# Expert rows added in memory by an accumulating scatter, and a last stage with fused sums that scales two tiles behind

## What is computed

```python
def expert_block(args):
    xblk, ex = args
    h = jax.nn.silu(xblk @ w_gate[ex]) * (xblk @ w_up[ex])
    return h @ w_down[ex]
...
return jnp.einsum("tkd,tk->td", y_slot.reshape(T, TOP_K, D), wts.astype(y_slot.dtype))
...
y_moe = _hier_moe(u, w_rg, w_re, w_e_gate, w_e_up, w_e_down)
x = _layer_norm(DEEPNORM_ALPHA * x + gate2 * y_moe, ln_g[1], ln_b[1])
```

## Time and profile before

| what | us |
|---|---|
| median of 3 runs | 1905.53 (1901.12 to 1906.41) |
| the profiled execution's own time | 1910.53 |
| its span, first to last instruction | 1908.8 |
| mixer stage | about 40 to 930 |
| output stage with routing | about 930 to 1250 |
| expert blocks, first to last scatter issued | 1284.3 to 1785.4 |
| combine stage | 1793.5 to 1908.8 |

### The profile page before, as it was taken

The page is one execution under the profiler, slowest core; times in us unless marked ns, Lnnn a source line. Parts: engine busy times, 40 slices in busy tenths (PEclk is TensorE's granted clock), DMA queues, the critical chain, the costliest instruction groups (busy, mean ns, idle before and its releaser), DMA issues. The chain is left out here.

```text
span 1908.8 us, 29069 instructions
## 1 busy us (share of the span) xinstructions
PE 1732.3 (91%) x8892; PEld 1341.6 (70%) x8893; DVE 1162.1 (61%) x1880; ACT 619.7 (32%) x770; POOL 585.8 (31%) x679
## 2 busy tenths in 40 slices
PE   5999999999999999999689999269999999999674
PEld 2777777777888799999468877246776776776321
DVE  3676666666666666666456887744565333455298
ACT  2333333223333322222211111123565334465233
POOL 0122222111222222012144556532443333343155
PEclk7999999999999899999799999579999999999897
DMA  6443334443333231322565342379899865797595
GB/s 251 160 135 128 113 120 144 134 144 110 97 105 94 72 100 51 101 95 58 177 196 175 128 138 100 100 239 342 295 380 361 283 217 176 267 323 289 215 390 176
DMA packets 171432, 342.72 MB, mean 180 GB/s; under 512 B 18932, under 2 KB 109844, under 8 KB 166335
## 3 DMA queue, kind: packets, MB, share of 16 engines
q1 hardware_dynamic: 148518, 285.35, 44.5%
q0 software_dynamic: 18000, 55.87, 8.0%
q10 hardware_dynamic: 4818, 0.26, 0.2%
HBM read 276.86 MB, written 64.58 MB: 179 GB/s over the span
## 5 line engine op out<-in xcount | busy, mean ns | idle before, releaser
L1532 DVE TENSOR_TENSOR w_gu_lo<-w_gu_raw,w_gu_hi (+1 forms) x64 | 146.5, 2292 | 146.9 <-ACT w_gu_hi L1525 141.7
L860 DVE TENSOR_TENSOR w_lo<-w_raw,w_hi 128x1024 fp32r<-128x1024 f32 x112 | 138.6, 1241 | 137.0 <-ACT w_hi L539 134.3
L651 POOL TENSOR_TENSOR o_r<-o_ms,neg_half 128x4 f32<-128x4 f32 (+1 forms) x16 | 16.8, 1051 | 640.6 <-DVEq L914 640.6
L685 PE MATMUL pr<-ua_hi,w_hi 128*128 128x512 f32 x448 | 185.0, 413 | 10.8 <-DVE ua_lo L865 10.8
L1920 PE MATMUL py<-w_dn_w,hhT 128*128 x400 | 183.2, 601 | 11.0 <-ACT hhT L1745 6.5
L685 PE MATMUL pr<-ub_hi,w_hi 128*128 128x288 f32 (+1 forms) x672 | 189.2, 335 | 0.0
L1881 PE MATMUL ph<-w_gu_hi,x_hi 128*128 (+1 forms) x408 | 183.4, 449 | 2.5 <-DVE x_lo L1784 2.5
L685 PE MATMUL pr<-ub_lo,w_hi 128*128 128x288 f32 (+1 forms) x672 | 183.8, 327 | 0.0
L685 PE MATMUL pr<-ub_hi,w_lo 128*128 128x288 f32 (+1 forms) x672 | 183.6, 327 | 0.0
L685 PE MATMUL pr<-ua_lo,w_hi 128*128 128x512 f32 x448 | 178.8, 399 | 0.0
L685 PE MATMUL pr<-ua_hi,w_lo 128*128 128x512 f32 x448 | 178.7, 399 | 0.0
(11 more groups left out here) (334 smaller groups left out, 3432.4 us busy)
## 6 DMA issues: line engine op xcount, KB each, us to landing
w_raw<-in_w_in SPq DMA_DIRECT2D x112, 512.0 KB, 4.1
w_gu_raw<-in_w_e_gate SPq DMA_DIRECT2D x32, 1024.0 KB
w_gu_raw<-in_w_e_up SPq DMA_DIRECT2D x32, 1024.0 KB
w_dn_w<-in_w_e_down SPq DMA_DIRECT2D x32, 1024.0 KB
w_mod<-in_w_mod_rest SPq DMA_DIRECT2D x16, 1024.0 KB
y_t<-y_scratch SPq DMA_DIRECT2D x16, 1024.0 KB, 7.5
w_ring<-in_w_mod_first SPq DMA_DIRECT2D x4, 2048.0 KB, 16.4
x_cols<-in_x_prompt_t SPq DMA_DIRECT2D x32, 256.0 KB, 4.9
```

The lines of the kernel that those rows point to most:

```text
L651: pool.tensor_tensor(o_r[:, 0:c], o_ms[:, 0:c], keep["neg_half"][:, 0:c], ALU.pow).then_inc(o_rs, 1)
L685: last = pe.matmul(pr[n % 2][:, a * 512:a * 512 + c], w[:, n % WS, k, :], x[:, k, a * c:(a + 1) * c], start=(k == 0 and m == 0), stop=(k = ...
L860: dve.tensor_tensor(w_lo[:, n % WS], w_raw[:, n % WRAW], w_hi[:, n % WS].bitcast(F32), ALU.subtract).then_inc(lo_done, 1)
L1532: dve.tensor_tensor(w_slot(keep["gu_lo"], s, lo, hi), w_slot(keep["gu_raw"], r, lo, hi), w_slot(keep["gu_hi"], s, lo, hi).bitcast(F32), AL ...
```

## The change

It does the following.

- The scatter of the expert stage adds to memory (`compute_op=ALU.add`), and both rows of token n have row n of y2 as destination; y2 has 2240 rows instead of 4352. Since an accumulation needs zeros to start from, 18 transfers of up to 512 KB (`clear_sums`) write zeros in units 10 to 15 of the mixer, from a tile that DVE clears once at the end of unit 9.
- In the combine stage one 512 KB load replaces the 1024 KB one, and tiles are loaded eight ahead instead of six. The PE step is gone. DVE's weigh reads the loaded tile in SBUF. The residual is scaled and added by one DVE operation from SBUF, which gives the row sums too (`accum_out`). ACT squares the centred tile with a row sum (`spread`) where it scaled the residual before; POOL makes variance plus epsilon of it. The two statistics operations and one small column leave DVE.
- `scale` and `shift` run two tiles behind instead of one, with three `z` and two `ps_n` tiles.

```diff
+        zero_rdy, zero_out = sem("zero_rdy"), sem("zero_out")
...
+        zeros = w_mod[:, :, :].rearrange("p k n -> p (k n)")[:, 0:D]
...
+                def clear_sums(i):
+                    n = min(P, NTOK + P - i * P)
+                    sp.wait_ge(zero_rdy, 1)
+                    sp.dma_start(scr["y2"][i * P:i * P + n, :], zeros[0:n, :]).then_inc(zero_out, 16)
...
+                    if u >= MOD_UNITS + 2:
+                        for i in range(3 * (u - MOD_UNITS - 2), 3 * (u - MOD_UNITS - 1)):
+                            clear_sums(i)
...
+                sp.wait_ge(zero_out, 16 * 3 * (UNITS - MOD_UNITS - 2))
...
+                    if u == MOD_UNITS + 1:
+                        dve.memset(zeros, 0.0).then_inc(zero_rdy, 1)
...
-                pool.iota(R["rows"][:, :, 0, 1], pattern=[[2 * P, T]], base=0, channel_multiplier=2)
-                pool.iota(R["rows"][:, :, 1, 1], pattern=[[2 * P, T]], base=1, channel_multiplier=2)
+                pool.iota(R["rows"][:, :, 0, 1], pattern=[[P, T]], base=0, channel_multiplier=1)
+                pool.iota(R["rows"][:, :, 1, 1], pattern=[[P, T]], base=0, channel_multiplier=1)
...
-                        dve.tensor_scalar(fill[:, :, 1], slot_i[:, :], 2 * NTOK, None, ALU.add)
+                        dve.tensor_scalar(fill[:, :, 1], slot_i[:, :], NTOK, None, ALU.add)
...
-                    pool.indirect_dma_start(scr["y2"], bass.IndirectOffsetOnAxis(ap=ids_cur[:, half, 1:2], axis=0), y_sb[:, half, :], None).then_inc(y_out, 16)
+                    pool.indirect_dma_start(scr["y2"], bass.IndirectOffsetOnAxis(ap=ids_cur[:, half, 1:2], axis=0), y_sb[:, half, :], None,
+                                            compute_op=ALU.add).then_inc(y_out, 16)
...
-    R = 6
+    R = 8
...
-        y2 = sb("y2_t", [P, R, 2, D])
+        y2 = sb("y2_t", [P, R, D])
         zw = sb("zw4", [P, D])
-        z = sb("z4", [P, 2, D])
+        z = sb("z4", [P, 3, D])
...
-        ps_x = ps("ps_x4", [P, D])
-        ps_n = ps("ps_n4", [P, D])
+        total, square = sb("total4", [P, 3]), sb("square4", [P, 3])
+        ve = sb("ve4", [P, 3])
+        rstd = sb("rstd4", [P, 3])
+        off = sb("off4", [P, 3])
+        nmean = sb("nmean4", [P, 3])
+        ps_n = [ps("ps_n0", [P, D]), ps("ps_n1", [P, D])]
+        ps_q = ps("ps_q4", [P, D])
...
                     if t >= R:
-                        sp.wait_ge(ysum, t - R + 1)
-                        sp.wait_ge(xa_rdy, t - R + 1)
-                    sp.dma_start(y2[0:n, s, :, :], scr["y2"][t * 2 * P:t * 2 * P + 2 * n, :].rearrange("(p k) d -> p k d", k=2)).then_inc(in_[s], 16)
+                        sp.wait_ge(weighed, t - R + 1)
+                        sp.wait_ge(z_rdy, t - R + 1)
+                    sp.dma_start(y2[0:n, s, :], scr["y2"][t * P:t * P + n, :]).then_inc(in_[s], 16)
                     sp.dma_start(x1[0:n, s, :], scr["x1"][t * P:t * P + n, :]).then_inc(in_[s], 16)
...
-                def residual(t):
-                    n = rows_of(t)
-                    act.wait_ge(in_[t % R], 32 * (t // R) + 32)
-                    if t:
-                        act.wait_ge(z_rdy, t)
-                    act.activation(ps_x[0:n, :], x1[0:n, t % R, :], ACT.Copy, scale=ALPHA).then_inc(xa_rdy, 1)
+                def spread(t):
+                    n, h = rows_of(t), t % 3
+                    act.wait_ge(mean_rdy, t + 1)
+                    act.activation(ps_q[0:n, :], z[0:n, h, :], ACT.Square, bias=nmean[0:n, h:h + 1], accum_out=square[0:n, h:h + 1])
+                    act.drain().then_inc(var_rdy, 1)
 
                 def centre(t):
-                    n, h = rows_of(t), t % 2
+                    n, h = rows_of(t), t % 3
                     act.wait_ge(off_rdy, t + 1)
-                    if t:
-                        act.wait_ge(zg_rdy, t)
-                    act.activation(ps_n[0:n, :], z[0:n, h, :], ACT.Identity, bias=off[0:n, h:h + 1], scale=rstd[0:n, h:h + 1]).then_inc(zn_rdy, 1)
-
...
+                    if t >= 2:
+                        act.wait_ge(zg_rdy, t - 1)
+                    act.activation(ps_n[t % 2][0:n, :], z[0:n, h, :], ACT.Identity, bias=off[0:n, h:h + 1], scale=rstd[0:n, h:h + 1]).then_inc(zn_rdy, 1)
+
                 for t in range(T):
+                    spread(t)
                     if t:
                         centre(t - 1)
-                    if t + 1 < T:
-                        residual(t + 1)
...
                 def root(t):
-                    n, h = rows_of(t), t % 2
+                    n, h = rows_of(t), t % 3
                     pool.wait_ge(var_rdy, t + 1)
+                    pool.tensor_scalar(ve[0:n, h:h + 1], square[0:n, h:h + 1], 1.0 / D, LN_EPS, ALU.mult, ALU.add)
+                    pool.drain()
                     pool.tensor_tensor(rstd[0:n, h:h + 1], ve[0:n, h:h + 1], keep["neg_half"][0:n, 0:1], ALU.pow)
                     pool.drain()
...
                     root(t)
-                    if t:
-                        shift(t - 1)
-
-            @block.tensor
-            def _(pe):
-                for t in range(T):
-                    n, s = rows_of(t), t % R
-                    pe.wait_ge(in_[s], 32 * (t // R) + 32)
                     if t >= 2:
-                        pe.wait_ge(weighed, t - 1)
-                    for k in range(2):
-                        for hf in range(2):
-                            last = pe.matmul(ps_y[t % 2][0:n, hf * 512:(hf + 1) * 512], keep["ident"][0:n, 0:n],
-                                             y2[0:n, s, k, hf * 512:(hf + 1) * 512], start=(k == 0), stop=(k == 1))
-                    last.then_inc(ysum, 1)
+                        shift(t - 2)
+                shift(LAST - 1)
...
                 def weigh(t):
                     n = rows_of(t)
-                    dve.wait_ge(ysum, t + 1)
-                    dve.tensor_tensor(zw[0:n, :], ps_y[t % 2][0:n, :], (gate_s if n < P else gate_p)[0:n, :], ALU.mult).then_inc(weighed, 1)
+                    dve.wait_ge(in_[t % R], 32 * (t // R) + 32)
+                    dve.tensor_tensor(zw[0:n, :], y2[0:n, t % R, :], (gate_s if n < P else gate_p)[0:n, :], ALU.mult).then_inc(weighed, 1)
 
                 def measure(t):
-                    n, h = rows_of(t), t % 2
-                    dve.wait_ge(xa_rdy, t + 1)
-                    dve.tensor_tensor(z[0:n, h, :], ps_x[0:n, :], zw[0:n, :], ALU.add)
+                    n, h = rows_of(t), t % 3
+                    if t >= 3:
+                        dve.wait_ge(zn_rdy, t - 2)
+                    dve.scalar_tensor_tensor(z[0:n, h, :], x1[0:n, t % R, :], ALPHA, zw[0:n, :], ALU.mult, ALU.add,
+                                             accum_out=total[0:n, h:h + 1])
                     dve.drain().then_inc(z_rdy, 1)
-                    for a in range(2):
-                        dve.bn_stats(stats[0:n, a, :], z[0:n, h, a * 512:(a + 1) * 512])
-                    dve.drain()
-                    dve.bn_aggr(mv[0:n, h, :], stats[0:n, :, :])
-                    dve.drain()
-                    dve.tensor_scalar(nmean[0:n, h:h + 1], mv[0:n, h, 0:1], -1.0, None, ALU.mult)
-                    dve.tensor_scalar(ve[0:n, h:h + 1], mv[0:n, h, 1:2], LN_EPS, None, ALU.add).then_inc(var_rdy, 1)
+                    dve.tensor_scalar(nmean[0:n, h:h + 1], total[0:n, h:h + 1], -1.0 / D, None, ALU.mult)
+                    dve.drain().then_inc(mean_rdy, 1)
...
                     if t >= 2:
                         dve.wait_ge(o_rdy, t - 1)
-                    dve.tensor_tensor(zg[0:n, t % 2, :], ps_n[0:n, :], ln2[0:n, 0, :], ALU.mult).then_inc(zg_rdy, 1)
-
...
+                    dve.tensor_tensor(zg[0:n, t % 2, :], ps_n[t % 2][0:n, :], ln2[0:n, 0, :], ALU.mult).then_inc(zg_rdy, 1)
...
                     dve.wait_ge(o_out[t % 4], 16 * (t // 4))
-                    dve.scalar_tensor_tensor(zg[0:n, h, :], z[0:n, h, :], mv[0:n, h, 0:1], ln2[0:n, 0, :], ALU.subtract, ALU.mult)
+                    dve.scalar_tensor_tensor(zg[0:n, t % 2, :], z[0:n, h, :], nmean[0:n, h:h + 1], ln2[0:n, 0, :], ALU.add, ALU.mult)
                     dve.wait_ge(off_rdy, t + 1)
                     dve.drain()
-                    dve.scalar_tensor_tensor(o[0:n, t % 4, :], zg[0:n, h, :], rstd[0:n, h:h + 1], ln2[0:n, 1, :], ALU.mult, ALU.add).then_inc(fin_rdy, 1)
+                    dve.scalar_tensor_tensor(o[0:n, t % 4, :], zg[0:n, t % 2, :], rstd[0:n, h:h + 1], ln2[0:n, 1, :], ALU.mult, ALU.add).then_inc(fin_rdy, 1)
...
                 for t in range(T):
                     weigh(t)
                     dve.drain()
+                    measure(t)
                     if t >= 2:
-                        dve.wait_ge(zn_rdy, t - 1)
-                    measure(t)
-                    if t:
-                        scale(t - 1)
+                        scale(t - 2)
+                scale(LAST - 1)
                 dve.wait_ge(o_rdy, LAST - 1)
                 finish(LAST)
...
```

(2 more changed lines are left out.)

21 lines of the change are left out of this document (3 added, 18 removed).

## The result

The changed kernel takes 1923.93 us (median of 4 runs, 1920.38 to 1926.06), the kernel before, run beside it, 1905.44 us (4 runs, 1901.12 to 1906.41): 1.0104 of its time, 95% interval 1.0083 to 1.0125. The change makes the kernel slower by 1%. The profiled execution took 1925.02 us, its span is 1923.4 us, 14.6 us over that of before.

The account below looks back on a forecast made before the run. Expert stage bound by PE on the mean, by full transfer queues in two stretches; combine stage by a DVE chain. Expert +27.7 and combine -9.8 sum to +17.9 us: 1928 profiled, 1923 against the median; 8-in-10 range 1893 to 1947.

Parts of the forecast that it names:

- Clearing, 0: Mixer: 18 added clearing transfers are hidden by PE and DVE and cost 0; were none hidden, 24 us.
- Adding, one pass of 1.46 us a scatter: Expert stage: each adding scatter costs one more pass, reaching PE where queues are full: 24.8 us, plus 1.5 us early.
- rival 1: Expert stage, full stretches: accumulation is free, total -9.8 us, 1896; chance 0.22.
- rival 3: Expert stage: accumulation costs two passes, +55.4 - 9.8 us, 1951; chance 0.12.
- Last landing, +1.4: End of the expert stage: the barrier waits for the last scatter, 1.4 us later.
- A landing some microseconds later doesn't hold POOL: Expert stage: each scatter waits for the one before, but with a block pitch of 10 us this holds nothing.
- Combine stage, start -6.9: Combine stage, first load to first `zw`: smaller first tile and no PE additions, 11.9 becomes 5.0 us.
- Interval 5.6, -7.1: Combine stage, `zw` to `zw`: DVE from two SBUF inputs and POOL exclude each other; 5.6 us each, sum 82.8 against 89.9.
- Rival 2: Combine stage: DVE and POOL don't exclude each other in the steady interval; stage gains 31.4 us, total -3.7, 1902; chance 0.12.
- End +4.2: Combine stage, last `zw` to the end: shifts, root, held finish operations and store take 17.7 us against 13.5.

Follow-up runs that it names:

- e8: The kernel before, unchanged, profiled once more: 1907.88 us (one run).
- e1: The changed kernel with the scatter writing instead of adding (a token's sum left out): 1890.21 us, 0.9939 of before.
- e9: The kernel before with adding scatters, even and odd blocks into two scratches so a scatter doesn't wait for the last one: 1929.82 us, 1.0125 of before.
- e6: The changed kernel with gate and up weights laid out in 8 KB runs instead of 1 KB: 1924.27 us, 1.0090 of before.
- e10: The changed kernel with GpSimd's copy of the next block's numbers into `ids_cur` moved ahead of the scatter: 1921.82 us, 1.0090 of before.
- e12: The changed kernel with `zw` in PSUM, gate and up weights in 8 KB runs and the early copy of `ids_cur`: 1895.00 us, 0.9953 of before.
- e3: The changed kernel with the tile `zw` in PSUM instead of SBUF, so that `z` has a PSUM input: 1908.45 us, 1.0024 of before.
- e5: The kernel before with gate and up weights laid out in 8 KB runs instead of 1 KB: 1911.89 us, 1.0044 of before.

## Why the prediction was right, step by step

The forecast was 1923 us and the direction slower; measured are 1923.93. By the two profiled executions the expert stage was forecast 5.5 us too dear, the last landing 2.3 us too cheap and the combine stage 2.5 us too dear; another 2.5 us lie ahead of the first scatter, where executions differ anyway.

- **Clearing, 0.** Held: PE in the mixer 874.08 of 890 us for 873.56, the 17 whole tiles cleared landing 5.9 us after issue at the median.
- **Adding, one pass of 1.46 us a scatter.** The queues were held 1.56 us more for each: the size is right, rival 1 (free) and rival 3 (two passes) fall. That the path felt it in full stretches only, 26.3 us, came as +20.8 us against the profile of before and as 24 to 28 us against e8 and e1, whose plain stages took 497.5 and 493.9. From the Trainium skill, "Collectives: The Full Stack", section "The bandwidth ceiling: the fold count and why AG ≠ RS ≠ AR", the estimate was 1.36 us and +25.8: this trace agrees in kind, at 1.56.
- **TensorE's clock, a term that the sum doesn't have.** The prediction lets each lateness reach PE and no more. Of the +20.8 us, 12.5 are PE standing still and 8.3 are its matmuls at a lower granted clock. That the sum came near is in part luck: the lateness was put too high and the clock at nothing.
- **Last landing, +1.4.** Mis-sized: 8.0 became 11.7 us, +3.7, in every kernel that adds. 0.6 us of it is the longer issue.
- **"A landing some microseconds later doesn't hold POOL".** This step failed. A landing is counted from the start of the issue. In the first full stretch it takes 9.6 us at the median, and the next scatter starts 0.8 to 0.9 us behind it: the three shown above start 10.42 and 10.51 us apart, where a block takes 10.0. So in full stretches GpSimd waited for its own last scatter. (What stands recorded with e9, issue 1.6 plus landing 8.9, counts the issue twice and comes to the same 10.5 by chance.) I had priced only the queue's way to PE, over the late weights. There is a second, over the copy of `ids_cur`; e6, e10 and e12 show that either alone is enough to hold the stage. It is in no term of the sum, which came out all the same; what it decides is the worth of a remedy: I had a single cause, and by it e6 should have gained 25 us.
- **Combine stage, start -6.9.** 11.9 became 4.5: -7.4.
- **Interval 5.6, -7.1.** 5.45 us, and 89.9 became 80.0: -9.9. The mechanism is the one laid out (`zw` ends 1.08 after the shift, forecast 1.07). The sum was 0.15 us too large in each interval, and the row sum costs 0.08. Rival 2 falls by the changed kernel's rows and by e3, where moving one operand out of SBUF took 15 us away. The estimate from the Trainium skill, "SBUF — State Buffer", section "SBUF: two separate sides", was 6.0: the measurement decides. The exclusion is there, but durations overlap at their ends.
- **End +4.2.** 13.5 became 18.5, +5.0. DVE's operation from two SBUF tiles took 3.34 us, held by the second of the two shifts.

The stage is 12.3 us shorter, not 9.8. The forecast +17.9 stands against +14.6 in span between the two profiled executions and +18.5 between the medians. The direction and the two costs are the mechanism laid out; that the total came within 1 us is luck, since errors of 2.3 to 5.5 us of both signs met in it.

**What stays open.** e5 made the kernel before slower by 0.4%, and its cause is not shown. Its profile has ScalarE's wait for `ids_cur` at 65.3 us (2.8 in e8), but that execution is the fastest of the seven (1904.86 us), and its 496.0 us from first to last scatter are no longer than e8's 497.5: a long wait of ScalarE's is no loss by itself. Packing together with the early copy and plain scatters wasn't tried. Of the 10 us between e12's 504.0 and e1's 493.9, 7.3 are TensorE standing still; how the waits for gathers, the queues and the chain of landings share them is not shown.
